# Forget gates of the recurrent mixer evicted as copies, their sigmoids taken later, and a rotation spread between index sums

## The chip, the cores and the metric

The kernel runs on one core of one Trainium2 chip. The metric is the device time of one execution in microseconds (us). The core has five engines that run their own instruction streams and wait for each other by semaphores: TensorE (PE in the profile; its weight loads are PEld), VectorE (DVE), ScalarE (ACT), GpSimd (POOL) and SyncE (SP), of which the last issues transfers only. All arithmetic is in fp32.

## What is computed

One step of two identical layers over 264 tokens: 256 of a prompt and one new token for each of 8 sequences. Each layer normalises its input, projects it by one wide matrix, and sends the parts to three mixers: a gated linear recurrence, a sparse attention whose keys an indexer picks, and an attention with compressed, selected and window keys. The part that the change touches, in short:

```
(hq, hf, hi, ..., dq, dk, dv, iq, ik, iw, ..., nq, nck, ...) = split(h @ w_in)
f   = lb + (1 - lb) * sigmoid(hf)          # forget gates, 4 heads of 128
hk  = (1 - lb) * sigmoid(-hf)
hqa = silu(hq)
dq, nq, dk, ... = rope(rms(...), qpos)     # queries and keys: root mean square, then rotation
score = sum_h iw_h * relu(iq_h . ik)       # the indexer's sum over 8 heads
```

`lb` is a bound for each channel. The rest (attention, recurrence, output gates, output projection) follows and isn't changed.

## The kernel before

Activations lie transposed, channels on the partitions and the 264 tokens in the free dimension. The projection is cut into slabs of 256 output columns (1 MB of weights each, three slots in SBUF) which stream in by SyncE's queue in a fixed order; a slot's next slab is sent when TensorE has finished the old one. Most slabs are two jobs of 128 columns. A job is 8 matmuls, shown as 16 records, into PSUM bank 0 or 1 in turn (line 902), and the job two further on may start only when ScalarE has evacuated the bank (`proj_free`). Seven slabs, among them `hf0`, are done by a scheme of seven products (line 921), whose sums VectorE forms. Everything is ordered by hand: each engine runs its own list, and every wait is written out.

The stretch around the change is the same in both layers. TensorE runs the last job pair `nq1`, the seven products of `hf0`, the sums of squares of the group `nq` (line 981), `hf1` (two jobs, heads 2 and 3 of the forget gates), `hq0` job 0, nine transposes of the values into token-major rows (line 1008, `rows`), `hq0` job 1, two transposes of the index weights (line 1016, `iw`), the first two index dots (lines 1024 and 1025), three tiny products (lines 1040 to 1043, `iwb`), `hq1` job 0, dots 2 and 3, the first key scores (line 1032), dots 4 and 5, `hq1` job 1, dots 6 and 7, and then `hi0` and `hi1` (line 914), with the recurrence's first products between them.

ScalarE meanwhile: the sigmoids of `hf0` (lines 1555 and 1557, once VectorE has formed its sums), `roots("nq")` (Ln at 1543 and Exp at 1545, which needs `zr dq`, the end of the `dq` rotation on VectorE, since both use the tile T1), then `evacuate("hf1")` (two sigmoids for each job straight out of PSUM, lines 1497 and 1498), `evacuate("hq0", 0)` (Silu, line 1523), the copies of `rows` (line 1564, recorded as 1460; their end is the mark `rows`), `evacuate("hq0", 1)`, the index weights, and the Relus of the index dots (line 1581). A function of another table set puts an ACT_TABLE_LOAD ahead of it.

VectorE: the rotation of `dq`, the rotation of `nq` in five steps (step 0 is four instructions at line 1931, steps 1 to 4 are one each at lines 1933, 1935, 1937 and 1939), then it waits for `rows`, builds small query tiles (QF at 1984 to 1986, `kn`, `vn`, QC at 1992) and `iwD` (line 1995), which `iwb` needs, and then adds up the index score, `acc 0` to `acc 7` (line 2011), each after its Relu; Relu n waits for acc n - 2. Then it scales the forget gates (lines 2032 and 2033, mark `f`), and a long chain of decays, merges and products (`decays`, `merge`, lines 2038 to 2195) gives the levels of the recurrence, with which TensorE interleaves further projection jobs.

Of the kernel before, what the change touches and what calls it, by code (L numbers as in the profile page):

```python
# [15 lines left out]
ACT = mybir.ActivationFunctionType  # L16
# [4 lines left out]
NS = 8  # L21
# [7 lines left out]
NH = 8  # L29
# [27 lines left out]
Z_IQ, Z_DQ, Z_NQ, Z_IK, Z_DK, Z_NCK, Z_NSK, Z_NWK, Z_NCV, Z_IW, Z_NWV, Z_DV, Z_NSV, Z_HQ = (  # L57
    0, 4, 8, 12, 13, 14, 15, 16, 17, 18, 19, 20, 21, 24)
# [249 lines left out]
def hybrid_step(nc, x_cols, pages_kv, page_table, state_win, win_k, win_v, state_hgrn, weights, small_w, cmp_w1,  # L308
                const, gate_rows, y_cols, z_keys, z_vals, p_hgrn, s_win, s_hgrn):
    ctx = ExitStack()  # L310
    with ctx:
# [16 lines left out]
        QC = sb("QC", [128, 2, NS * (ROWS + NH)])  # L328
# [27 lines left out]
        def at(off, *shape, rows=128):  # L356
            n = int(np.prod(shape))
            assert off + n <= ARENA, (off, shape)
            v = arena[0:rows, off:off + n]
            if len(shape) == 2:  # L360
                v = v.rearrange("p (a b) -> p a b", a=shape[0])
            if len(shape) == 3:
                v = v.rearrange("p (a b c) -> p a b c", a=shape[0], b=shape[1])
            if len(shape) == 4:
                v = v.rearrange("p (a b c d) -> p a b c d", a=shape[0], b=shape[1], c=shape[2])
            return v


        Z = at(0, NZ, LT)
# [10 lines left out]
        iwS = at(13664, NS)  # L380
        RI = at(14112, PAST // 2)
        ikT = at(14112, 4, PAST)
        iwD = at(19528, NS, NH)[0:NS]
        iwP = at(19592, 2, NH)
        i2 = at(19608, 64)[0:NS]
        SQ = (at(18208, 5, LT), at(22168, 4, LT))
        T1 = at(19528, 5, LT)
        T2 = at(20848, 5, LT)
# [5 lines left out]
        kT = at(23360, 4, LT)  # L394
        fT = at(24416, 4, LT)
# [161 lines left out]
        halves = (slice(0, HD), slice(HD, 128))  # L557
# [296 lines left out]
        def _(pe):  # L854
# [16 lines left out]
            for l in range(DEPTH):  # L871
# [139 lines left out]
                project("hq0", 1)  # L1011

                pe.wait_ge(rows_a.sem, rows_a(l, "rows"))
                pe.wait_ge(grp_v.sem, grp_v(l, "zr nq"))
                for t in range(2):
                    last = nc.tensor.transpose(ps[:, 2, t * NH:t * NH + NH], Z[0:NH, Z_IW, t * 128:t * 128 + 128], ident[0:NH, 0:NH])
                last.then_inc(pidx_p.sem, pidx_p.mark("iw"))
# [438 lines left out]
        def _(act):  # L1456
# [14 lines left out]
            for l in range(DEPTH):  # L1471
# [17 lines left out]
                def evacuate(name, only=None):  # L1489
                    for j, job in enumerate(SLAB_OF[name][2]):  # L1490
                        if only not in (None, j):
                            continue
                        n = JOB_AT[name, j]
                        act.wait_ge(proj_ready, l * NJOB + (n + 1))
                        src = ps[0:min(job[3], 128), n % 2, 0:LT]
                        if job[0] == "F":
                            A(fT[:, job[1], :], src, ACT.Sigmoid)
                            A(kT[:, job[1], :], src, ACT.Sigmoid, scale=-1.0).then_inc(proj_free, 1)  # L1498
                            continue
                        if job[0] == "S":  # L1500
                            for i in range(4):
                                last = copy(HVs[eight[i], :], ps[eight[i], n % 2, 0:128])
                            last.then_inc(proj_free, 1)
                            continue
                        if name == "ikw":
                            b, i, _ = SQUARES[Z_IK]
                            for h in halves:
                                copy(Z[h, Z_IK, :], ps[0:HD, n % 2, 0:LT])
                                A(SQ[b][h, i, :], ps[0:HD, n % 2, 0:LT], ACT.Square)
                            copy(Z[0:56, Z_IW, :], ps[HD:120, n % 2, 0:LT]).then_inc(proj_free, 1)  # L1510
                            continue
                        if job[0] == "Y":
                            copy(Y[:, job[1] // 4, job[1] % 4, :], src).then_inc(proj_free, 1)
                            continue
                        if job[1] in SQUARES and job[0] == "T":
                            b, i, group = SQUARES[job[1]]
                            copy(Z[:, job[1], :], src)
                            A(SQ[b][:, i, :], src, ACT.Square).then_inc(proj_free, 1)
                            if job[1] == (Z_NWK if group == "k" else GROUPS[group][0] + 3):
                                act.drain().then_inc(grp_a.sem, grp_a.mark(f"sq {group}"))  # L1520
                            continue
                        if job[0] == "T":
                            A(Z[0:job[3], job[1], :], src, ACT.Silu if name[:2] == "hq" else ACT.Copy).then_inc(proj_free, 1)
                            continue
                        w, o = job[3], job[4]
                        copy(HV[:, :, o:o + w], ps[:, n % 2, :].rearrange("p (t c) -> p t c", t=2)[:, :, 0:w]).then_inc(proj_free, 1)
# [11 lines left out]
                def roots(name):  # L1538

                    n = GROUPS[name][1]  # L1540
                    act.wait_ge(grp_p.sem, grp_p(l, f"ss {name}"))
                    act.wait_ge(grp_v.sem, grp_v(l, f"zr {BEFORE[name]}"))
                    A(T1[:, 0:n, :], ps[:, 2:2 + n, 0:LT], ACT.Ln, bias=epsb[:, :])
                    act.drain()
                    A(T1[:, 0:n, :], T1[:, 0:n, :], ACT.Exp, scale=-0.5).then_inc(grp_a.sem, grp_a.mark(f"rs {name}"))

                for name in FRONT[2:]:
                    if name in SEVEN:
                        squares(SEVEN.index(name))
                    elif name in SLAB_OF:  # L1550
                        evacuate(name)
                    elif name[:2] == "ss":
                        roots(name[3:])
                act.wait_ge(sv_v.sem, sv_v(l, "c 6"))
                A(kT[:, 0:2, :], fT[:, 0:2, :], ACT.Sigmoid, scale=-1.0)
                act.drain()
                A(fT[:, 0:2, :], fT[:, 0:2, :], ACT.Sigmoid)
                roots("nq")
                evacuate("hf1")
                evacuate("hq0", 0)  # L1560
                act.wait_ge(rows_p.sem, rows_p(l, "rows"))
                for t in range(3):
                    n = 128 if t < 2 else NS
# [226 lines left out]
        def _(ve):  # L1790
# [53 lines left out]
            for l in range(DEPTH):  # L1844
# [77 lines left out]
                def rotation(name, step):  # L1922

                    z, n, _, cols = GROUPS[name]
                    x, turned, kept = Z[:, z:z + n, :], T2[:, 0:n, :], T1[:, 0:n, :]
                    ve.drain()
                    if step == 0:
                        ve.wait_ge(grp_a.sem, grp_a(l, f"rs {name}"))
                        for i in range(n):
                            c = cols[i]  # L1930
                            STT(Z[:, z + i, :], Z[:, z + i, :], gains[:, c:c + 1], T1[:, i, :], ALU.mult, ALU.mult)
                    if step == 1:
                        nc.vector.stream_shuffle(turned, x, ROTATED)
                    if step == 2:
                        TT(kept, x, cosb(n), ALU.mult)
                    if step == 3:
                        TT(turned, turned, sinb(n), ALU.mult)
                    if step == 4:
                        TT(x, kept, turned, ALU.add).then_inc(grp_v.sem, grp_v.mark(f"zr {name}"))
# [31 lines left out]
                third_bank(6)  # L1971
                for step in range(1, 5):
                    rotation("dq", step)
                for step in range(5):
                    rotation("nq", step)


                ve.wait_ge(rows_a.sem, rows_a(l, "rows"))
# [3 lines left out]
                for g, h in enumerate(halves):  # L1982
                    hh = slice(4 * g, 4 * g + 4)
                    TC(qf[0:HD, 0, :, hh], Z[h, Z_IQ:Z_IQ + 4, seq_cols].rearrange("p j s -> p s j"))
                    TC(qf[h, 1, :, hh], Z[h, Z_DQ:Z_DQ + 4, seq_cols].rearrange("p j s -> p s j"))
                    TC(qf[h, 2, :, hh], Z[h, Z_NQ:Z_NQ + 4, seq_cols].rearrange("p j s -> p s j"))
                for i, z in enumerate((Z_DK, Z_NSK, Z_NWK)):
                    TC(kn[:, i, :], Z[:, z, seq_cols])
                TC(vn[:, :, :], vrow[0:NS, 2, :].rearrange("p (i c) -> p i c", i=3))
                ve.drain()  # L1990
                for a in range(2):
                    TC(QC[:, a, :].rearrange("p (b x) -> p b x", b=NS)[:, :, 0:NH], qf[:, 1 + a, :, :])
                ve.drain().then_inc(sidx_v.sem, sidx_v.mark("qf"))
                i8 = ident[0:NS, 0:NH]
                TT(iwD, Z[0:NH, Z_IW, seq_cols].unsqueeze(2).to_broadcast([NH, NS, NH]), i8.unsqueeze(1).to_broadcast([NH, NS, NH]), ALU.mult)\
# [12 lines left out]
                for n, h in enumerate(HEADS):  # L2008
                    ve.wait_ge(pidx_a.sem, pidx_a(l, f"relu {n}"))
                    for t, c in enumerate((slice(0, 128), slice(128, 384))):  # L2010
                        STT(acc[:, c], RL[:, n % 2, c], iwP[:, t, h:h + 1], causal[:, c] if n == 0 else acc[:, c], ALU.mult, ALU.add)
                    ve.drain().then_inc(pidx_v.sem, pidx_v.mark(f"acc {n}"))

                def top_keys(c):

# [506 lines left out]
```

## Time and profile before

| | |
|---|---|
| median of 3 runs | 930.22 us (929.90 to 933.64) |
| profiled execution | 933.25 us, of which the span is 931.6 us |
| TensorE busy | 912.0 us, 98% of the span |
| VectorE, ScalarE busy | 554.0 us (59%), 296.5 us (32%) |
| mean granted TensorE clock | 0.989 of full speed |
| chain that ended last, by engine | TensorE 86%, VectorE 6%, ScalarE 4% |

The busy shares say which engine has work, not what one stage waits for; the waits and the timeline of a stretch say that. In the chain that ended last each row is a piece of work and begins where the one before it released it, so rows there don't overlap. In a timeline a row is a run of like instructions of one engine, and the end of one can lie up to 0.2 us behind the start of the next, since instructions are pipelined. Square brackets give idle time of the engine before the row and what ended it. The granted clock is a share of full speed: 1.00 is 2.4 GHz and 0.50 is 1.2 GHz.

### The profile page before, as it was taken

The page shows a single profiled execution, that of the slowest core. Times are in us where ns is not written, and L with a number is a line of the kernel's source. Part 1 is how long each engine was busy: PE and PEld are TensorE (multiplying, and loading weights), DVE is VectorE, ACT ScalarE, POOL GpSimd, SP SyncE. Part 2 cuts the span into 40 slices and gives each one's busy share as a digit, 9 for nine tenths or more (in the row PEclk, how much of TensorE's full clock was granted, in tenths as well). Part 3 has the DMA queues.
Part 4 walks back from the last instruction along what each step waited for, and adds up shares of the span by engine and source line. Part 5 has one row for each costly group of instructions (what it writes and reads, how often), then busy time and mean ns, then how long its engine had stood idle before and what let it go on. Part 6 is the DMA issues. An engine that isn't in the chain of part 4 may idle for free.

```text
span 931.6 us, 18064 instructions
## 1 busy us (share of the span) xinstructions
PE 912.0 (98%) x6588; PEld 753.9 (81%) x6588; DVE 554.0 (59%) x1538; ACT 296.5 (32%) x631; POOL 130.0 (14%) x258
## 2 busy tenths in 40 slices
PE   9999899999999999999999989999999999999998
PEld 8998578878777777888899977788777777778887
DVE  5886578876744677034258755888676436751331
ACT  3134433246733113400120363422576321243000
POOL 0420000002033262000060000000110323600000
PEclk9999899999999999999999999999999999999999
DMA  8654456317189799334465443572261997973432
GB/s 293 231 171 147 155 205 258 136 57 272 46 296 381 249 386 335 116 136 156 160 197 173 162 147 121 228 269 91 92 237 56 361 384 268 381 259 140 136 135 92
DMA packets 56794, 189.05 MB, mean 203 GB/s; under 512 B 9218, under 2 KB 22914, under 8 KB 44418
## 3 DMA queue, kind: packets, MB, share of 16 engines
q1 hardware_dynamic: 43426, 138.56, 42.4%
q0 software_dynamic: 12992, 49.16, 14.1%
q8 instruction: 52, 0.85, 0.4%
q14 instruction: 36, 0.29, 0.1%
q10 hardware_dynamic: 288, 0.18, 0.1%
HBM read 177.47 MB, written 18.77 MB: 211 GB/s over the span
## 4 chain that ended last, share of the span: by engine, by line
PE 86%; DVE 6%; ACT 4%; DVEq 2%; issue 1%; ACTq 0%
PE ps L1114 18%; PE ps L902 11%; PE ps L1436 9%; PE ps L921 9%; PE ps L1330 6%; PE ps L1448 3%; PE ps L1442 3%; PE ps L914 3%; PE ps L1309 2%; PE ps L1235 2%; PE ps L1410 2%; PE ps L1224 2%; DVE arena L2091 1%; PE ps L966 1%; PE ps L1202 1%
## 5 line engine op out<-in xcount | busy, mean ns | idle before, releaser
L902 PE MATMUL ps<-hT,slab 128*128 128x264 f32 (+1 forms) x736 | 176.6, 397 | 8.8 <-ACT arena L1498 8.8
L1114 PE MATMUL ps<-hT,slab 128*128 128x264 f32 x736 | 175.8, 396 | 0.1
L902 PEld LDWEIGHTS ps<-hT,slab 128*128 128x128 f32 (+1 forms) x736 | 140.6, 194 | 35.5 <-issue 10.7
L1114 PEld LDWEIGHTS ps<-hT,slab 128*128 128x128 f32 x736 | 139.4, 193 | 30.8 <-DVEq L2245 3.2
L1460 ACT ACTIVATE arena<-ps 128x512 f32<-128x512 f32 (+21 forms) x134 | 62.6, 497 | 125.4 <-PE ps L1330 47.5
L1436 PE MATMUL ps<-Y,slab 128*128 128x264 f32 x384 | 85.8, 386 | 0.0
L1436 PEld LDWEIGHTS ps<-Y,slab 128*128 128x128 f32 x384 | 72.8, 190 | 12.3
L1330 PEld LDWEIGHTS ps<-arena,w 128*128 128x128 f32 x512 | 58.4, 192 | 10.0 <-issue 6.6
L1330 PE MATMUL ps<-arena,w 128*128 128x128 f32 x512 | 61.4, 278 | 0.0
L620 POOL DMA_DIRECT2D arena<-in_pages_kv_dram x64 | 33.4, 522 | 151.7 <-DVEq L2475 114.5
L629 POOL DMA_DIRECT2D arena<-in_pages_kv_dram x64 | 35.1, 549 | 99.6 <-PE ps L1330 27.0
L1663 ACT ACTIVATE arena<-arena,st 128x128 f32<-128x128 f32 (+1 forms) x96 | 42.4, 443 | 12.0 <-DVEq L2245 11.0
L1614 ACT ACTIVATE arena<-ps 128x264 f32<-128x264 f32 x38 | 14.8, 389 | 80.3 <-PE ps L1114 80.0
L634 POOL DMA_DIRECT2D arena<-in_pages_kv_dram x64 | 35.1, 549 | 11.7 <-PE ps L1330 9.2
L2462 DVE TENSOR_TENSOR xT<-xT,ps 128x264 f32<-128x264 f32 x16 | 6.9, 429 | 44.4 <-PE ps L1442 23.8
L1460 ACT ACTIVATE Y<-ps 128x264 f32<-128x264 f32 x24 | 9.4, 390 | 72.0 <-PE ps L902 72.0
L2099 DVE MAX8 tk<-tk 104x8 f32<-104x257 f32 x64 | 27.4, 429 | 4.3
L921 PE MATMUL ps<-arena,slab 128*128 128x132 f32 x224 | 29.8, 276 | 0.0
L1479 ACT ACTIVATE arena<-xT 128x264 f32<-128x264 f32 x16 | 6.3, 420 | 72.1 <-DVE xT L2462 67.5
L1442 PE MATMUL ps<-arena,slab 128*128 128x264 f32 x128 | 28.8, 386 | 0.0
L1448 PE MATMUL ps<-arena,slab 128*128 128x264 f32 x128 | 28.8, 386 | 0.0
L914 PE MATMUL ps<-slab,hT 128*128 128x256 f32 x128 | 28.5, 381 | 0.0
(397 smaller groups left out, 1460.1 us busy)
## 6 DMA issues: line engine op xcount, KB each, us to landing
slab<-in_weights_dram SPq DMA_DIRECT2D x84, 1024.0 KB, 5.1
arena<-in_pages_kv_dram SPq DMA_DIRECT2D x64, 256.0 KB, 8.3
arena<-in_pages_kv_dram POOLq DMA_DIRECT2D x64, 256.0 KB, 6.8
arena<-in_pages_kv_dram POOLq DMA_DIRECT2D x64, 128.0 KB, 8.3
arena<-in_pages_kv_dram SPq DMA_DIRECT2D x64, 128.0 KB, 11.9
out_dram<-in_state_win_dram POOLq DMA_DIRECT2D x2, 4088.0 KB, 24.1
arena<-in_state_hgrn_dram SPq DMA_DIRECT2D x2, 2048.0 KB, 11.6
out_dram<-arena POOLq DMA_DIRECT2D x2, 2048.0 KB, 8.9
```

The costliest lines, as they stand in the source:

```text
L629: engine.dma_start(KB[u % 4][:, e, k, :], page_of("keys", l, pages[u // 2 + NPAIR * e, 4 * (u % 2) + k])).then_inc(page_in[u % 4][odd], 16)
L634: engine.dma_start(V[:, s, i, :, :].rearrange("p a c -> p (a c)"), page_of("vals", l, pages[s, i])).then_inc(v_in[odd], 16)
L902: last = mm(ps[0:job[3], n % 2, 0:LT], v[:, k, job[2]:job[2] + job[3]], hT[:, k, :], start=(k == 0), stop=(k == KD - 1))
L914: last = mm(ps[:, n % 2, t * 256:t * 256 + width], hT[:, k, t * 128:t * 128 + 128], v[:, k, o:o + width], start=(k == 0), stop=(k == KD - 1))
L921: last = mm(out, x[:, k, :], y[:, k, :], start=(k == 0), stop=(k == 3))
L1114: last = mm(ps[:, bank, 0:LT], v[:, k, (d % 2) * 128:(d % 2) * 128 + 128], hT[:, k, :], start=(k == 0), stop=(k == KD - 1))
L1330: last = mm(out[:, kv, :, 64 * hf:64 * hf + 64], w1[:, kv, t, :], blocks[:, :, o:o + 2 * NPB8], start=(t == 0), stop=(t == ST - 1))
L1436: last = mm(ps[:, d % 4, 0:LT], v[:, j, dd * 128:dd * 128 + 128], Y[:, a, j, :], start=(j == 0), stop=(j == 3))
L1442: last = mm(ps[:, 4 + d, 0:LT], views[d // 2][:, k, (d % 2) * 128:(d % 2) * 128 + 128], mT[:, k, :], start=(k == 0), stop=(k == KD - 1))
L1448: last = mm(ps[:, d - 4, 0:LT], v[:, k, (d % 2) * 128:(d % 2) * 128 + 128], mT[:, k, :], start=(k == 0), stop=(k == KD - 1))
L1460: return A(out, in_, ACT.Copy, scale=scale)
L1663: A(x[:, j, :], x[:, j, :], ACT.Exp, scale=-1.0, bias=st[:, c + j:c + j + 1], accum_out=sa[:, c + j:c + j + 1])
```

## The change

- ScalarE copies `hf1` raw out of PSUM into the tile fT in place of four sigmoids. The copy of job 0 stands ahead of `roots("nq")`, that of job 1 behind it.
- The sigmoids of `hf0` are not taken ahead of the roots. All four heads are taken at once (kT from fT with scale -1, then fT in place, 128x1056 each), behind the Silu of `hq0` job 0 and ahead of the copies of `rows`.
- VectorE does steps 0 and 1 of the `nq` rotation where it did all five. Steps 2 and 3 go behind `acc 1`, and step 4 behind `acc 5`, followed by the QF copies of `dq` and `nq` and the two QC copies that were made ahead of `iwD`.
- TensorE doesn't wait for the end of the `nq` rotation (`zr nq`) ahead of the `iw` transposes, and `iwD`, `iwP` and `i2` move to a place in the arena that the rotation doesn't use.

```diff
@@ buffers
-        iwD = at(19528, NS, NH)[0:NS]
-        iwP = at(19592, 2, NH)
-        i2 = at(19608, 64)[0:NS]
+        iwD = at(30000, NS, NH)[0:NS]
+        iwP = at(30064, 2, NH)
+        i2 = at(30080, 64)[0:NS]
@@ TensorE
                 pe.wait_ge(rows_a.sem, rows_a(l, "rows"))
-                pe.wait_ge(grp_v.sem, grp_v(l, "zr nq"))
@@ ScalarE, evacuate
                         if job[0] == "F":
-                            A(fT[:, job[1], :], src, ACT.Sigmoid)
-                            A(kT[:, job[1], :], src, ACT.Sigmoid, scale=-1.0).then_inc(proj_free, 1)
+                            copy(fT[:, job[1], :], src).then_inc(proj_free, 1)
                             continue
@@ ScalarE, order
+                evacuate("hf1", 0)
+                roots("nq")
+                evacuate("hf1", 1)
+                evacuate("hq0", 0)
                 act.wait_ge(sv_v.sem, sv_v(l, "c 6"))
-                A(kT[:, 0:2, :], fT[:, 0:2, :], ACT.Sigmoid, scale=-1.0)
                 act.drain()
-                A(fT[:, 0:2, :], fT[:, 0:2, :], ACT.Sigmoid)
-                roots("nq")
-                evacuate("hf1")
-                evacuate("hq0", 0)
+                A(kT, fT, ACT.Sigmoid, scale=-1.0)
+                act.drain()
+                A(fT, fT, ACT.Sigmoid)
                 act.wait_ge(rows_p.sem, rows_p(l, "rows"))
@@ VectorE
-                for step in range(5):
-                    rotation("nq", step)
+                rotation("nq", 0)
+                rotation("nq", 1)
                 ...
                     TC(qf[0:HD, 0, :, hh], Z[h, Z_IQ:Z_IQ + 4, seq_cols].rearrange("p j s -> p s j"))
-                    TC(qf[h, 1, :, hh], Z[h, Z_DQ:Z_DQ + 4, seq_cols].rearrange("p j s -> p s j"))
-                    TC(qf[h, 2, :, hh], Z[h, Z_NQ:Z_NQ + 4, seq_cols].rearrange("p j s -> p s j"))
                 ...
-                ve.drain()
-                for a in range(2):
-                    TC(QC[:, a, :].rearrange("p (b x) -> p b x", b=NS)[:, :, 0:NH], qf[:, 1 + a, :, :])
                 ve.drain().then_inc(sidx_v.sem, sidx_v.mark("qf"))
                 ...
                     ve.drain().then_inc(pidx_v.sem, pidx_v.mark(f"acc {n}"))
+                    if n == 1:
+                        rotation("nq", 2)
+                        rotation("nq", 3)
+                    if n == 5:
+                        rotation("nq", 4)
+                        ve.drain()
+                        for g, h2 in enumerate(halves):
+                            hh = slice(4 * g, 4 * g + 4)
+                            TC(qf[h2, 1, :, hh], Z[h2, Z_DQ:Z_DQ + 4, seq_cols].rearrange("p j s -> p s j"))
+                            TC(qf[h2, 2, :, hh], Z[h2, Z_NQ:Z_NQ + 4, seq_cols].rearrange("p j s -> p s j"))
+                        ve.drain()
+                        for a in range(2):
+                            TC(QC[:, a, :].rearrange("p (b x) -> p b x", b=NS)[:, :, 0:NH], qf[:, 1 + a, :, :])
```

## Rows read from the trace of the kernel before

**Rows 1.** Busy time and share of every engine, from the page
```profile
PE 912.0 (98%) x6588; PEld 753.9 (81%) x6588; DVE 554.0 (59%) x1538; ACT 296.5 (32%) x631; POOL 130.0 (14%) x258
```

**Rows 2.** Waits of TensorE: total us, times, longest
```profile
PE ps L902 <- ACT arena L1498: 8.8, 2, 4.4
PE ps L1093 <- DVEq L2195: 2.0, 2, 1.0
```

**Rows 3.** Chain that ended last, 66 to 145 us: start us, us, what
```profile
97.88 6.14 PE ps L902 x16
104.01 0.98 PE ps L1008 x9
104.99 3.56 PE ps L902 x16
108.56 0.22 PE ps L1016 x2
...
109.64 0.20 PE ps L1040 x2
...
132.47 6.91 PE ps L914 x32
```

**Rows 4.** Timeline of TensorE: start us, busy us, line, operation, count, idle before
```profile
86.20 7.28 PE L902 MATMUL ps<-hT,slab 128*128 128x264 f32 x32
```

**Rows 5.** Timeline of ScalarE, layer 0, same columns
```profile
90.89 1.28 ACT L1543 ACT_TABLE_LOAD   x1 [4.21 <-DVE arena L1939]
...
94.67 1.08 ACT L1545 ACTIVATE arena<-arena 128x1056 f32<-128x1056 f32 x1
...
98.32 1.28 ACT L1523 ACT_TABLE_LOAD   x1
104.05 0.39 ACT L1523 ACTIVATE arena<-ps 128x264 f32<-128x264 f32 x1 [4.45 <-PE ps L902]
105.03 1.22 ACT L1460 ACTIVATE arena<-ps 128x384 f32<-128x384 f32 x3 [0.59 <-PE ps L1008]
```

**Rows 6.** Timeline of VectorE, layer 0, same columns
```profile
95.78 1.71 DVE L1931 SCALAR_TENSOR_TENSOR arena<-arena,small 128x264 f32<-128x264 f32 x4 [4.97 <-ACT arena L1545]
...
101.67 1.26 DVE L1939 TENSOR_TENSOR arena<-arena 128x1056 f32<-128x1056 f32 x1
106.34 0.06 DVE L1796 MEMSET spare<- 128x1 f32 x1 [3.41 <-ACTq L1565]
...
107.58 0.34 DVE L1989 COPY vn<-arena 8x384 f32<-8x384 f32 x1
...
108.41 0.21 DVE L1995 TENSOR_TENSOR arena<-arena,cst 8x64 f32<-8x64 f32 x1
...
115.43 1.61 DVE L2011 SCALAR_TENSOR_TENSOR arena<-arena 128x128 f32<-128x128 f32 x4 [2.57 <-ACT arena L1581]
...
121.92 1.61 DVE L2011 SCALAR_TENSOR_TENSOR arena<-arena 128x128 f32<-128x128 f32 x4 [3.01 <-ACT arena L1581]
```

**Rows 7.** TensorE in windows of 1 us: busy, granted clock, DMA share, GB/s
```profile
96.00:97.00 1.00, 0.00 (x0) 0.50 1.00 426
...
102.00:103.00 1.00, 1.00 (x5) 0.69 0.00 0
...
202.00:203.00 1.00, 0.50 (x3) 1.00 0.00 0
...
297.00:298.00 1.00, 1.00 (x3) 0.59 1.02 357
```

**Rows 8.** Timeline of TensorE around two thin stretches of layer 0
```profile
202.50 0.31 PE L1183 MATMUL ps<-cst,arena 104*128 104x104 f32 x1 [0.71 <-ACT arena L1460]
...
294.32 1.93 PE L1282 MATMUL ps<-arena 15*64 15x512 f32 x8
...
296.94 5.51 PE L1114 MATMUL ps<-hT,slab 128*128 128x264 f32 x16
```

**Rows 9.** Timeline of the SyncE queue: start us, us, line, transfer
```profile
108.59 0.33 SPq L688 DMA_DIRECT2D slab<-in_weights_dram  x1
```

## The prediction

> **What bounds the kernel now.** I read the page first. TensorE is busy 98% of the span, so only its idle time, its time at the lower clock and its own work can give anything [rows 1]. The waits of TensorE come next, and nearly half of its 20 us of idle time is one wait: job 0 of `hq0` waits for ScalarE's second sigmoid of `hf1`, line 1498, twice (once a layer), 4.4 us each [rows 2]. The next largest is 1.0 us a layer. Third, the chain that ended last, around that wait: the job behind the wait takes 6.14 us, where the same 16 records take 3.56 us a little later [rows 3]. The windows of 1 us say why: the granted clock is 0.50 (1.2 GHz) from 96 us on, after TensorE stood still from 93.5 us, and full (2.4 GHz) again within the window 102 to 103 [rows 7]. So the wait costs 4.39 us of standing and 2.58 us of slow matmuls, about 7.0 us a layer, 14 us in all.
>
> What ended the wait is ScalarE's timeline. It can't take the roots of `nq` before 90.89 us, because the `dq` rotation holds T1; two table loads, Ln and Exp follow and end at 94.67 + 1.08 = 95.75; and only then come a third load and the sigmoids that free bank 1 [rows 5]. But job 0 of `hf1` had been done since 86.20 + 3.56 = 89.76 us [rows 3, 4], with ScalarE idle for 4.21 us until 90.89 [rows 5].
>
> **The change part by part** (times of layer 0; layer 1 has the same shape).
>
> *Copies in place of sigmoids.* The copy of `hf1` job 0 (0.39 us, as the 128x264 Silu [rows 5]) fits into the idle 4.21 us, at 89.8 to 90.2. It frees bank 1, and `hq0` job 0 starts straight behind `hf1`, at 86.20 + 2 x 3.56 = 93.32, in place of 97.88. At full clock it ends at 96.88. The `rows` transposes wait for the roots (95.75), which is earlier, and end at 96.88 + 0.98 = 97.86; `hq0` job 1 follows and ends at 97.86 + 3.56 = 101.42 [rows 3]. Its bank is free at 96.2. In the trace of before it ended at 108.56, so TensorE is 7.14 us ahead here, which is the 4.39 and the 2.58 and 0.17 of overlap between matmuls.
>
> *What is late next: ScalarE's `rows`.* The work taken from ahead of the wait now stands ahead of the `rows` copies. From 95.75: copy of `hf1` job 1 0.39; load for Silu 1.28; Silu 0.39; load for Sigmoid 1.28; two sigmoids of 128x1056, each as the Exp of that shape, 1.08; three copies of `rows` 1.22 [rows 5]. The sum is 6.72 us, and two drains make it about 6.8: `rows` is marked at about 102.55 us (before: 105.03 + 1.22 = 106.25 [rows 5]). TensorE comes to its wait for it at 101.42, so a new wait of about 1.15 us takes the place of the old one. Queued behind it on TensorE are `iw` and the first dots, 109.64 - 108.56 = 1.08 us [rows 3], which end at 103.7.
>
> *VectorE's small tiles.* `iwb` needs `iwD`. Before, it was done at 108.41 + 0.21 = 108.62, 2.37 us after `rows` [rows 5, 6]. The change takes four of six QF copies from that path (the six, a memset and part of `kn` fill the 1.24 us from 106.34 to 107.58, some 0.12 each with a gap saved, so 0.5 us) and the QC copies with their drain (from 107.92 to 108.41 is 0.49, of which a drain of 0.1 stays) [rows 6]. That leaves about 1.5 us: `iwD` at 102.55 + 1.5 = 104.05, another wait of about 0.35 us. `iwb` then starts at about 104.1 in place of 109.64. **The shift is 5.5 us a layer, 11.0 us in all.** Rotation steps 0 and 1 end at 95.78 + 1.71 + 1.33 = 98.8, well ahead of `rows`, and taking away the wait for `zr nq` gives nothing in itself: the rotation would have ended by 101.67 + 1.26 = 102.93 [rows 6], 0.4 us behind `rows`.
>
> *The third load.* `hq0` job 1 now needs a Silu load again, behind `rows`: 102.6 + 1.28 + 0.39 = 104.3 [rows 5]. That is before `iwb` is out, so the Relus, which wait for `iwb`, don't move against it.
>
> *Deferred steps.* Steps 2 and 3 of the rotation are 2 x 1.33 = 2.7 us (1.26 and a gap) behind `acc 1`, where VectorE sat idle 2.57 us before `acc 2`; and Relu 4, the first that needs `acc 2`, waits for TensorE longer than the 0.1 us left over. Step 4, four copies and two QC copies are 1.3 + 0.6 + 0.4 = 2.3 us behind `acc 5`, where the idle time before `acc 6` was 3.01 us [rows 6]. Both are hidden. Without this cover the 5.0 us would go to the mark `f` and from there to the chain of levels, which is what TensorE waits for at line 1093, 1.0 us a layer [rows 2]. With the cover, `f` moves by the same 5.5 us as TensorE, and so does all that follows; the transfers are sent on TensorE's marks and move with it. The slab of `hi1` is sent on the end of `hq0`, so at 101.4 in place of 108.59 [rows 9], 7.1 us earlier, for a use that moves from 132.5 by 5.5 (the row of line 914) [rows 3]; the 16 index-key transfers behind it on SyncE's queue gain as much.
>
> *Edits that cost nothing:* new addresses for `iwD`, `iwP` and `i2` add no wait.
>
> *The clock.* This is the unknown term. From 101.4 to about 104.7 us TensorE would have no dense matmul: 1.15 us of waiting, 1.1 us of 8-row and 64-row products, 0.35 us of waiting, 0.6 us of tiny products. The clock fell after the wait of 4.39 us; it also fell with no wait at all, at 297 us, behind 2.5 us of products with 15 and 24 rows, and the job at 296.94 took 5.51 us, where one of this shape takes half of 7.28, so 1.9 us more [rows 4, 7, 8]. It did not fall at 202 to 203 us, where thin products and 0.71 us of waiting make a stretch of about the same length [rows 7, 8]. So the new stretch costs 0 to 1.9 us a layer. The same fall at 297 us was there in both layers of this execution. It may be gone in another, which would give up to 3.8 us back, and that the profiled execution is 3.03 us above the median fits this, though only one trace shows it. Against the profiled 933.25 us the sum is thus 933.25 - 11.0 = 922.25, with 0 to 3.8 us to add and 0 to 3.8 to take off; against the median, 930.22 - 11.0 = 919.2 with 0 to 7.6 to add. I take one low stretch, 1.9 us: 921.1 us. The stretches at 202 us and at 297 us are about equally near to the new one, so about half of the places is what I go by, less one, as the median execution seems to have had none at 297 us.
>
> *A rule against the change.* The trace shows 1.28 us for each table load, with the next ACTIVATE right behind it [rows 5], and the change puts Silu, Sigmoid and Silu in a row, two more switches than grouping would need. The Trainium skill, "ScalarE: Activation LUTs", section "What ACT_TABLE_LOAD costs", counts a drain of about 1.38 us beside each load of 1.28 us, and its rules say to do all of one set before switching. By the page the two loads ahead of `rows` would cost 2.76 us a layer more and the sum would be an estimated 926.6. The trace doesn't agree: from 90.89 to 94.67 are 3.78 us for a load, an Ln of the Exp's size and a second load, 1.28 + 1.1 + 1.28, which leaves 0.1 us for drains [rows 5].
>
> **The rivals.**
> *1. ScalarE is later than summed.* Each microsecond by which `rows` is late is one on TensorE, since TensorE waits for it already. If what stands ahead of `rows` costs two more table loads' worth, 2 x 1.28 = 2.6 us a layer, the result is 921.1 + 5.1 = 926.2. Against it: every piece has its own duration in the rows, and the loads are all 1.28 us. The table rule of the page is of this kind.
> *2. Clock low in most places.* All four possible low stretches (the new one and that at 297 us, in each layer) give 919.2 + 7.6 = 926.8; three give 924.9. For it: the new stretch is longer than either row that I compare it with. Against it: the one at 202 us did nothing.
> *3. Slower: the clock stays low.* The place is from `iwb` on. At 0.50 each microsecond of full-speed matmuls costs one more, so from 5.5 us of them at the lower clock a layer gains nothing. If it stayed low through both `hq1` jobs and `hi0`, some 14 us of such work, a layer would lose 8.5 us, and the result would be 947. Against it: the longest low stretch in the rows is from 96 to 102.6 us, and it ended under dense matmuls, as these are.
> *4. No effect.* The wait only moves: the level chain on VectorE, busy throughout, is as late as before, because the deferred 5.0 us land in it. Then a layer gains 5.5 - 5.0 = 0.5 us, and the result is 929 to 930. Against it: the idle times of 2.57 and 3.01 us [rows 6].
> *5. More.* The sigmoids or small tiles cost less, and no low stretch comes: 916 to 918.5.
>
> **How the numbers follow.** Forecast, 919 to 923.5 (none to two low stretches): 0.62. Rival 1: 0.08. Rival 2: 0.13. Rival 3: 0.02. Rival 4: 0.06. Rival 5: 0.09. The predicted time is 921.1. The range 918.0 to 926.0 holds the forecast, the three-stretch case and about half of rivals 1 and 5, a little over 0.8. A measurement of this kernel can tell about 0.5% (4.65 us) from no change: faster means below 925.6. Faster: 0.62 + 0.09 + most of rival 2 and half of rival 1 = 0.86. Within: 0.11. Slower: 0.03.
>
> **What the profile after would show.** The wait of `hq0` on ScalarE gone; `hq0` job 0 straight behind `hf1` in 3.56 us; a wait of about 1.2 us at line 1016 ended by ScalarE's `rows` copies and one of about 0.35 us at line 1040 ended by VectorE; `acc 2` and `acc 6` not later against their Relus; the granted clock around 102 to 109 us either full or with one low stretch that costs up to 1.9 us; the wait at line 1093 still 1.0 us. The prediction is wrong if `rows` comes after about 103.5 us, if Relu 4 or 6 waits for VectorE, or if the level chain starts to hold TensorE for longer.

## The result and the profile after

| | before | after |
|---|---|---|
| median | 931.93 us (929.90 to 935.99, 4 runs) | 922.48 us (919.95 to 924.44, 4 runs) |
| profiled execution | 933.25 us, span 931.6 | 921.3 us, span 919.6 |
| mean granted TensorE clock | 0.989 | 0.998 |
| TensorE busy | 912.0 us | 905.0 us |

The ratio is 0.9883, with a 95% interval of 0.9853 to 0.9913: some 11 us faster (8 to 14 us by the interval; the medians of the table are 9.4 us apart). Two more comparisons of the same kernel, on other occasions, gave 0.9875 (0.9850 to 0.9901) and 0.9864 (0.9833 to 0.9895).

The waits of TensorE after the change (engine and line, what it waited for: us in total, times, longest). The line numbers of TensorE's part are one lower than before.

```profile
PE ps L1092 <- DVEq L2203: 2.1, 2, 1.1
PE ps L1015 <- ACTq L1565: 1.8, 2, 0.9
...
PE ps L1039 <- DVE arena L1990: 0.7, 2, 0.3
```

The 8.8 us of [rows 2] are gone. In their place stand two short waits: at the `iw` transposes for ScalarE's mark `rows`, 0.9 us a layer, and at `iwb` for VectorE's `iwD`, 0.34 us. The wait in the level chain is what it was, 1.0 us a layer [rows 2].

The timeline of TensorE in layer 0. In this execution the layer begins 0.65 us later than in the one of before (86.85 against 86.20 [rows 4]), so 0.65 is to be taken off each time:

```profile
86.85 10.84 PE L902 MATMUL ps<-hT,slab 128*128 128x264 f32 x48
97.53 1.15 PE L1008 MATMUL ps<-cst,arena 128*128 128x128 f32 x9
98.51 3.73 PE L902 MATMUL ps<-hT,slab 128*128 128x264 f32 x16
103.15 0.29 PE L1015 MATMUL ps<-cst,arena 8*128 8x8 f32 x2 [0.91 <-ACTq L1565]
...
104.64 0.27 PE L1039 MATMUL ps<-arena,cst 8*8 8x64 f32 x2 [0.34 <-DVE arena L1990]
...
105.26 3.83 PE L902 MATMUL ps<-hT,slab 128*128 128x264 f32 x16
```

The same timeline of the kernel before, from `hq0` job 0 on:

```profile
97.88 6.14 PE L902 MATMUL ps<-hT,slab 128*128 128x264 f32 x16 [4.39 <-ACT arena L1498]
...
109.57 0.27 PE L1040 MATMUL ps<-arena,cst 8*8 8x64 f32 x2
...
110.19 3.83 PE L902 MATMUL ps<-hT,slab 128*128 128x264 f32 x16
```

After the change the first row is 48 records long: both jobs of `hf1` and job 0 of `hq0` run in one piece, 10.84 us, at full clock. Before, `hq0` job 0 alone took 6.14 us behind 4.39 us of waiting. `iwb` starts at 104.64 - 0.65 = 103.99 in place of 109.57, a shift of 5.58 us a layer. `hq1` job 0 behind it is 5.58 us earlier too (105.26 - 0.65 = 104.61 in place of 110.19). The chain [rows 3] puts `iwb` of before at 109.64; only timelines are compared here.

ScalarE in the same stretch:

```profile
90.61 0.39 ACT L1459 ACTIVATE arena<-ps 128x264 f32<-128x264 f32 x1 [8.96 <-PE ps L902]
91.52 1.28 ACT L1541 ACT_TABLE_LOAD   x1 [0.52 <-DVE arena L1939]
...
95.30 1.08 ACT L1543 ACTIVATE arena<-arena 128x1056 f32<-128x1056 f32 x1
96.29 0.38 ACT L1459 ACTIVATE arena<-ps 128x264 f32<-128x264 f32 x1
96.69 1.28 ACT L1521 ACT_TABLE_LOAD   x1
97.98 0.39 ACT L1521 ACTIVATE arena<-ps 128x264 f32<-128x264 f32 x1
98.44 1.28 ACT L1558 ACT_TABLE_LOAD   x1
99.73 1.08 ACT L1558 ACTIVATE arena<-arena 128x1056 f32<-128x1056 f32 x1
100.88 1.08 ACT L1560 ACTIVATE arena<-arena 128x1056 f32<-128x1056 f32 x1
101.87 1.20 ACT L1459 ACTIVATE arena<-ps 128x384 f32<-128x384 f32 x3
103.17 1.28 ACT L1521 ACT_TABLE_LOAD   x1
```

The first copy sits in 8.96 us of idle time, where before the sigmoids of `hf0` and a table load stood. From the end of the roots (95.30 + 1.08) to the end of the copies of `rows` (101.87 + 1.20) it is a queue 6.7 us long, with no gap over 0.1 us, of which 2.56 us are table loads. Each ACTIVATE begins 0.01 us behind its load.

And VectorE's index sums with the deferred steps between them:

```profile
107.18 0.75 DVE L2006 SCALAR_TENSOR_TENSOR arena<-arena 128x128 f32<-128x128 f32 x2
108.10 1.26 DVE L1935 TENSOR_TENSOR arena<-arena,cst 128x1056 f32<-128x1056 f32 x1 [0.17 <-issue]
109.44 1.26 DVE L1937 TENSOR_TENSOR arena<-arena,cst 128x1056 f32<-128x1056 f32 x1
110.62 3.36 DVE L2006 SCALAR_TENSOR_TENSOR arena<-arena 128x128 f32<-128x128 f32 x8
114.16 1.26 DVE L1939 TENSOR_TENSOR arena<-arena 128x1056 f32<-128x1056 f32 x1 [0.17 <-issue]
...
116.15 0.38 DVE L2020 COPY QC<-QF 128x64 f32<-128x64 f32 x2
116.99 1.61 DVE L2006 SCALAR_TENSOR_TENSOR arena<-arena 128x128 f32<-128x128 f32 x4 [0.46 <-ACT arena L1581]
```

`acc 2` to `acc 5` run in one piece (3.36 us, eight records) straight behind rotation steps 2 and 3: of the idle 2.57 us ahead of `acc 2` [rows 6] nothing is left, and `acc 2` comes 5.46 us earlier than before where TensorE is 5.58 us earlier, so 0.12 us late. Ahead of `acc 6` 0.46 us of the 3.01 us of idle time [rows 6] are left. The deferred steps fit, with little to spare.

### The profile page after: what moved, and what is told of

It is laid out like the page before. It is cut to its first block, busy times and chain, and to the rows that moved or that the text cites. A ratio compares the mean times of both kernels' runs of the same rounds, so it can differ in the third digit from the quotient of the medians.

```text
span 919.6 us, 18062 instructions
## 1 busy us (share of the span) xinstructions
PE 905.0 (98%) x6588; PEld 750.0 (82%) x6588; DVE 553.8 (60%) x1538; ACT 297.1 (32%) x627; POOL 129.7 (14%) x258
## 4 chain that ended last, share of the span: by engine, by line
PE 84%; DVE 7%; ACT 3%; DVEq 2%; issue 2%; DMA 1%; ACTq 0%; SPq 0%
PE ps L1113 18%; PE ps L902 9%; PE ps L1435 9%; PE ps L921 9%; PE ps L1329 7%; PE ps L1447 3%; PE ps L1441 3%; PE ps L914 3%; PE ps L1308 2%; PE ps L1234 2%; PE ps L1409 2%; PE ps L1223 2%; DVE arena L2099 1%; PE ps L1201 1%; PE ps L891 1%
## 5 line engine op out<-in xcount | busy, mean ns | idle before, releaser
L902 PE MATMUL ps<-hT,slab 128*128 128x264 f32 (+1 forms) x736 | 171.4, 389 | 0.0
L902 PEld LDWEIGHTS ps<-hT,slab 128*128 128x128 f32 (+1 forms) x736 | 137.7, 190 | 24.4 <-issue 1.1
L1459 ACT ACTIVATE arena<-ps 128x512 f32<-128x512 f32 (+12 forms) x138 | 64.1, 494 | 142.6 <-PE ps L1329 47.2
```

The costliest lines, as they stand in the source:

```text
L902: last = mm(ps[0:job[3], n % 2, 0:LT], v[:, k, job[2]:job[2] + job[3]], hT[:, k, :], start=(k == 0), stop=(k == KD - 1))
L1459: return A(out, in_, ACT.Copy, scale=scale)
```

## The experiments

My theory: the copy of `hf1` job 0 ahead of the roots takes away a wait and with it the lower clock behind it; what is left is set, one for one, by what stands ahead of ScalarE's `rows` and of VectorE's `iwD`. All ratios are to the kernel before, timed beside them. The runs follow the theory's steps. Rows are of layer 0 unless it is said otherwise.

**The change again.**

> The change itself, once more, as the yardstick of the runs beside it. About 9 to 11 us below the kernel before (0.988 to 0.990). Its trace should again show the two new waits, 0.91 us at the iw transposes and 0.34 us at iwb, a layer.

Measured: 921.03 us against 932.95, 0.9875 (0.9850 to 0.9901), at the good end of what was expected. The waits are 1.8 and 0.7 us in all, as above.

**The wait parted from the clock.** The kernel before, with nine spare products in the wait, whose results nothing uses:

```diff
                 project("hf1", 1)
+                for _ in range(9):
+                    mm(ps[:, 7, 0:LT], ident, hT[:, 0, :], start=True, stop=True)
                 project("hq0", 0)
```

> The kernel before, with nine spare 264-column products into the unused bank 7 behind hf1, about 4.0 us of work in the wait of 4.39 us (results unused). It parts the price of the wait from that of the lower clock. My theory: the clock stays at 2.4 GHz, hq0 job 0 takes 3.6 us in place of 6.14, and the time falls by 2 x 2.5 = 5 us, to about half of the gain of the change, with no wait taken away. The rival, the slow job has another cause (banks, transfers): no gain, or a small loss if the spare products run past the wait.

Measured: 928.68 us against 932.85, 0.9942 (0.9919 to 0.9964), 4 to 5 us faster with nine products more in each layer (18 records). The timeline of its TensorE:

```profile
87.67 7.28 PE L902 MATMUL ps<-hT,slab 128*128 128x264 f32 x32
94.80 4.17 PE L1003 MATMUL ps<-hT,cst 128*128 128x264 f32 x18
99.35 3.80 PE L902 MATMUL ps<-hT,slab 128*128 128x264 f32 x16 [0.39 <-ACT arena L1500]
```

Job 0 of `hq0` starts 11.68 us behind the start of `hf1` (99.35 - 87.67), to the hundredth as before (97.88 - 86.20 [rows 4]), since ScalarE has not changed. But it takes 3.80 us in place of 6.14. The mean granted clock of this execution is 1.000, against 0.989. The lower clock was thus a cost of its own, 2.3 us a layer, and the cause was TensorE standing still. About 5 of the change's 11 to 12 us are this.

**The two halves of the change.** First ScalarE's half alone (VectorE's list as before: five rotation steps, six QF copies and two QC copies ahead of `iwD`; the new addresses and the removed wait stay).

```diff
-                rotation("nq", 0)
-                rotation("nq", 1)
+                for step in range(5):
+                    rotation("nq", step)
```

> The change with VectorE's list put back: all five steps of the nq rotation, all QF and QC copies ahead of iwD. My theory: ScalarE's part frees the bank and carries the gain; VectorE's part is only there to keep iwD early. rows comes at about 102.5 us but the rotation ends about 0.5 us later, then 2.3 us to iwD in place of 1.45 us: iwb 1.3 us a layer later than in the change, 2.6 us in all, so about 8 us below the kernel before. Rival A, the moved passes carry a good part of the gain: less than 5 us below before. Rival B, they give nothing: as the change.

Measured: 927.4 us (924.2 to 932.9) against 932.95, 0.9931 (0.9909 to 0.9954). That is 5.5 us, half of the change's gain, less than the 8 us that I expected, and nearer to the bound that I had set for rival A. The timeline of its TensorE, and the windows of 1 us (length, busy, granted clock, DMA share, GB/s):

```profile
103.09 0.29 PE L1015 MATMUL ps<-cst,arena 8*128 8x8 f32 x2 [0.92 <-ACTq L1565]
...
105.81 0.38 PE L1039 MATMUL ps<-arena,cst 8*8 8x64 f32 x2 [1.57 <-DVE arena L1995]
...
106.74 6.63 PE L902 MATMUL ps<-hT,slab 128*128 128x264 f32 x16
```

```profile
104.00:105.00 1.00, 0.24 (x4) 1.00 0.98 352
105.00:106.00 1.00, 0.19 (x2) 0.81 0.93 385
106.00:107.00 1.00, 1.00 (x9) 0.50 0.85 286
...
112.00:113.00 1.00, 1.00 (x5) 0.78 0.13 35
```

The second wait is 1.57 us, 1.23 more than in the change, as the theory has it. But the clock fell here, behind two waits of 0.92 and 1.57 us with thin products between them, in both layers: `hq1` job 0 took 6.63 us in place of 3.83, so 2.8 us more on top of 1.23, and the tiny products ahead of it another 0.3 us. This execution took 932.9 us; the best one, 924.2 us, was 8.7 us below before, as expected without that fall. Its mean granted clock was 0.998, that of the other two 0.993. An estimate: one stretch at half clock as long as the one here (6.8 us) takes 0.0037 off the mean, and one as short as that at 297 us before (3.4 us) 0.0018. This profile has two of each kind (0.989), and two short ones alone would leave 0.996, so 0.993 needs at least one of the long ones. The fall was thus in three of the four executions.

VectorE's half alone (the kernel before, with VectorE's list, the addresses and the removed wait of the change):

> The kernel before with VectorE's part of the change, the new addresses and no wait for zr nq, and ScalarE's list as before. My theory: nothing, within 0.3 us of before, since before the change iwD was done 1 us ahead of TensorE and the rotation 3 us ahead of rows. The rival, the shorter path to iwD or the removed wait is worth something on its own: 1 to 2 us faster; or the deferred steps cost something: slower by up to 6 us.

Measured: 932.73 us against 932.85, 1.000 (0.9983 to 1.0018). Its TensorE waits at `hq0` as before:

```profile
PE ps L902 <- ACT arena L1497: 8.8, 2, 4.4
```

Nothing, as expected. VectorE's half is worth nothing by itself and about half of the gain beside the other, part of it by the clock, since it decides only when `rows` is early. The deferred steps cost nothing either.

**What sets the new waits.** Twice more sigmoids ahead of `rows`:

```diff
                 A(kT, fT, ACT.Sigmoid, scale=-1.0)
                 act.drain()
+                A(kT, fT, ACT.Sigmoid, scale=-1.0)
+                act.drain()
+                A(kT, fT, ACT.Sigmoid, scale=-1.0)
+                act.drain()
                 A(fT, fT, ACT.Sigmoid)
```

> The change with the sigmoid of kT done three times over (same result), 2 x 1.15 us more ahead of the rows copies. My theory of one for one: the wait at iw grows from 0.91 to about 3.2 us a layer, 4.6 us in all, and since TensorE then stands for over 3 us, the clock falls there too and costs up to 1.9 us more a layer: 4.6 to 8.4 us above the change. The rival, that the new wait has slack in what follows (the level chain on VectorE sets the end anyway): less than 3 us above the change.

Measured: 931.4 us against 932.85, 0.9982 (0.9968 to 0.9996), so 10 us above the change by the ratios, more than the 4.6 to 8.4 that I expected. Its TensorE in layer 0:

```profile
105.29 0.28 PE L1015 MATMUL ps<-cst,arena 8*128 8x8 f32 x2 [3.22 <-ACTq L1569]
...
107.66 6.80 PE L902 MATMUL ps<-hT,slab 128*128 128x264 f32 x16
```

The wait grew from 0.91 to 3.22 us, which is one for one with 2.3 us of work, and the job behind it took 6.80 us in place of 3.83. The two together are 5.3 us a layer. The price of the clock, 3 us, is over the upper end that I had given, 1.9 us, and this is what the expectation had too small.

Less work ahead of `rows`: the sigmoids of `hf0` stay in the idle time ahead of the roots, and only heads 2 and 3 are taken late.

```diff
+                act.wait_ge(sv_v.sem, sv_v(l, "c 6"))
+                A(kT[:, 0:2, :], fT[:, 0:2, :], ACT.Sigmoid, scale=-1.0)
+                act.drain()
+                A(fT[:, 0:2, :], fT[:, 0:2, :], ACT.Sigmoid)
                 evacuate("hf1", 0)
                 roots("nq")
                 ...
-                act.wait_ge(sv_v.sem, sv_v(l, "c 6"))
                 act.drain()
-                A(kT, fT, ACT.Sigmoid, scale=-1.0)
+                A(kT[:, 2:4, :], fT[:, 2:4, :], ACT.Sigmoid, scale=-1.0)
                 act.drain()
-                A(fT, fT, ACT.Sigmoid)
+                A(fT[:, 2:4, :], fT[:, 2:4, :], ACT.Sigmoid)
```

> The change, but the sigmoids of hf0 (heads 0 and 1) stay where they were, in ScalarE's idle time ahead of the roots, and only heads 2 and 3 are taken behind the Silu, 128x528 each (0.64 us) in place of 128x1056 (1.08 us). My theory: what stands ahead of the rows copies sets the new wait one for one, so it shrinks by 0.88 us a layer, from 0.91 to about 0.05, and the time by 1.8 us against the change. The rival, the wait is set by something else (the transposes, a drain, a table load): no change.

Measured: 918.91 us (918.38 to 919.34) against 932.95, 0.9850 (0.9834 to 0.9867), 2.1 us below the change beside it. In layer 0:

```profile
102.18 0.29 PE L1015 MATMUL ps<-cst,arena 8*128 8x8 f32 x2 [0.36 <-ACTq L1568]
```

The wait fell from 0.91 to 0.36 us in layer 0, and in layer 1 nothing but a gap of 0.04 us is left of it, as expected. In layer 0 of this execution the roots began 0.33 us later, counted from `hf1` (91.43 - 86.43 = 5.00 us, against 91.52 - 86.85 = 4.67 in the change), and 0.91 - 0.88 + 0.33 is 0.36. So the wait follows the queue to the hundredth, and taking all four heads at once is the part of the change that costs something. Why the roots began later here stays open.

All four sigmoids behind Relu 1, and the evacuation of `hq1` job 0 behind Relu 5:

```diff
                 evacuate("hq0", 0)
-                act.wait_ge(sv_v.sem, sv_v(l, "c 6"))
-                act.drain()
-                A(kT, fT, ACT.Sigmoid, scale=-1.0)
-                act.drain()
-                A(fT, fT, ACT.Sigmoid)
                 act.wait_ge(rows_p.sem, rows_p(l, "rows"))
                 ...
                 relus(1)
-                evacuate("hq1", 0)
+                act.wait_ge(sv_v.sem, sv_v(l, "c 6"))
+                act.drain()
+                A(kT, fT, ACT.Sigmoid, scale=-1.0)
+                act.drain()
+                A(fT, fT, ACT.Sigmoid)
                 for n in range(2, 6):
                     relus(n)
+                evacuate("hq1", 0)
                 evacuate("hq1", 1)
```

> The change, but all four sigmoids stand behind Relu 1, with rows copied straight behind the first Silu, and hq1 job 0 evacuated behind Relu 5. The count of table loads stays. My theory: both new waits go (0.91 and 0.34 us a layer), 2.5 us below the change, so 11.5 to 13.5 us below the kernel before, and the chance of a low clock behind them goes too. The rival, the wait moves again: Relus 2 to 5 now wait for the sigmoids, and acc and the dots with them, which gives the 2.5 us back or more.

> The change again in five rounds, beside the kernel with late sigmoids on the same chip: 0.986 to 0.990 of before.

> The kernel with late sigmoids again in five rounds. My theory: 2.5 us below the change beside it (the two new waits of 1.25 us a layer gone), 0.983 to 0.987 of before. The rival, that the first result was luck in where the clock fell: as the change, within 1 us.

Measured: 917.96 us and 0.9846 (0.9824 to 0.9867) in the first comparison. In the second, of more rounds, it was 916.85 us and 0.9814 (0.9786 to 0.9841), beside 920.68 us and 0.9864 for the change. It beats both kernels: 3 to 4 us below the change, where 2.5 us were expected; the intervals of the two kernels overlap a little in both comparisons. The timeline of TensorE, from the first comparison, has no wait between `hf1` and `hi0`:

```profile
85.95 10.84 PE L902 MATMUL ps<-hT,slab 128*128 128x264 f32 x48
96.63 1.15 PE L1008 MATMUL ps<-cst,arena 128*128 128x128 f32 x9
97.61 3.73 PE L902 MATMUL ps<-hT,slab 128*128 128x264 f32 x16
101.27 0.29 PE L1015 MATMUL ps<-cst,arena 8*128 8x8 f32 x2
...
102.35 0.27 PE L1039 MATMUL ps<-arena,cst 8*8 8x64 f32 x2
...
102.97 3.83 PE L902 MATMUL ps<-hT,slab 128*128 128x264 f32 x16
...
115.27 7.17 PE L914 MATMUL ps<-slab,hT 128*128 128x256 f32 x32
```

And that of `hi0` in the change:

```profile
117.38 7.17 PE L914 MATMUL ps<-slab,hT 128*128 128x256 f32 x32
```

From the start of `hf1` to that of `hq1` are 17.02 us, against 18.41 in the change and 23.99 before, so 1.4 us a layer less than in the change. Up to `hi0` they are 29.32 us, against 30.53: 0.2 us are given back at dots 4 and 5, and 1.2 us a layer, 2.4 in all, stay. That is the size that was expected; the rest of the 3 to 4 us is within the intervals.

**The cover of the deferred steps.** In the change, rotation steps 2 to 4 and the copies in one piece behind `acc 7`, ahead of the mark `f`:

> The change with VectorE's deferred steps 2 to 4 and the copies put behind acc 7 in one piece, where no idle time covers them: 4.9 us straight ahead of the mark f. My theory: f is 4.9 us later, of which some 2 us are slack ahead of the first recurrence products and the chain of levels; the rest, about 3 us a layer, appears as waits of TensorE in the levels: about 6 us above the change. The rival that the chain of levels has more slack than that: within 1 us of the change. The rival that it has none: 10 us above, so no gain over the kernel before.

Measured: 928.87 us against 932.85, 0.9954 (0.9934 to 0.9974), so 7 to 8 us above the change. The waits of its TensorE:

```profile
PE ps L1062 <- DVEq L2042: 5.6, 2, 2.9
PE ps L1092 <- DVEq L2202: 2.1, 2, 1.1
```

A wait of 2.8 us a layer appeared at line 1062, the recurrence's first products, which need `f`. The levels, line 1092, wait for no longer than before. So the size was right, 5 us of work less 2 us of slack, and the place was not: I had put it into the chain of levels. The lower clock came behind this wait as well:

```profile
127.99 3.44 PE L1062 MATMUL ps<-arena 128*128 128x128 f32 x16 [2.94 <-DVEq L2042]
...
585.53 3.78 PE L1062 MATMUL ps<-arena 128*128 128x128 f32 x16 [2.71 <-DVEq L2042]
...
589.10 8.38 PE L914 MATMUL ps<-slab,hT 128*128 128x256 f32 x32
```

In the change the products of line 1062 take 2.05 us and the job pair behind them 7.07. So the clock cost 1.4 us in layer 0 and 1.7 + 1.3 = 3.0 us in layer 1. With the waits that is 10.1 us, where the span of this execution is 9.4 us above that of the change beside the first experiments (928.9 against 919.5): the wait and the clock account for all of it.

## Why the prediction was right, point by point

The forecast was 921.1 us, within 918 to 926; the median came out at 922.48. The mechanism was right; that the number came so near is in part luck, as the last points say.

- **What bounds.** Right. The one wait of 4.39 us and the slow job behind it were what the change took away, and the spare products showed the two prices apart, 2.3 us for the clock against the 2.58 that I read.
- **The shift.** 5.5 us a layer forecast, 5.58 measured, and so still at the first products of the recurrence (125.50 - 0.65 in place of 130.42). Job 0 of `hq0` starts straight behind `hf1`.
- **ScalarE late next.** The sum of 6.72 us plus drains was 6.7 us in the trace. The wait was forecast at 1.15 us and is 0.91; I counted 0.1 us for drains that overlap the next work, and a job by the 3.56 us of the chain, though its end as TensorE's next wait sees it is 0.17 later. The experiments with more and with less in the queue moved the wait the way the sum has it.
- **VectorE's small tiles.** 0.35 us forecast, 0.34 measured.
- **Deferred steps.** Covered, as forecast, but for the 0.12 us of `acc 2`, which reached no wait of TensorE: 0.46 us of cover were left ahead of `acc 6`, where I had 0.7. The idle time ahead of Relus 4 and 6 is ended by TensorE, after 1.00 and 0.46 us, as before. Rival 4 (no effect) needed them to land in the level chain, whose wait is 1.0 us a layer as before. What happens without cover was right in size and wrong in place.
- **The clock.** This term was kept open, and one low stretch was taken. In the profiled execution of the change the only one was again behind the 15-row and 24-row products, in layer 0, and the new place had none in the three profiled executions of the change. The other two had no low stretch at all. Over all 14 timed executions of the change the mean granted clock was 0.996 to 1.000, where four low stretches gave 0.989 with ScalarE's half alone, so rival 2 (low in most places) is out. The 1.9 us that I charged to the new place are thus shown by no run of the change. The upper end was too low besides: where the clock does fall in the new place, the job behind it costs 2.7 to 3.0 us, not 1.9, since the clock then stays low for longer (from about 105.6 to 112.4 us with ScalarE's half alone, against 297.2 to 300.6 before). The nearer row was that of the wait itself, 96 to 102.6 us and 2.58 us, which I had read. Why a stretch is short or long stays open: with the deferred steps uncovered, the same products behind nearly the same wait met a low stretch of 3.4 us in layer 0 and of 6.8 us in layer 1.
- **The base.** 930.22 us was low for the kernel before; further runs gave medians of 931.9 to 933.7. It was 1.7 us below the median of the first comparison, and the 1.9 us for a low stretch made up for it by luck. The 9.1 us of gain that the forecast has from it compare with 9.4 between the medians of the first comparison and 12 to 13 in the two later ones, and the shift by itself, 2 x 5.58 = 11.2 us, is nearer to these.
- **The rule on table switches.** The Trainium skill, "ScalarE: Activation LUTs", section "What ACT_TABLE_LOAD costs", would put 1.38 us of drain beside each load of 1.28 us. The loads here take 1.28 us, each begins within 0.1 us of the end of the ACTIVATE before it, and the next ACTIVATE starts 0.01 us behind, so the trace doesn't agree on the drain. The advice of its section "Rules for kernel authors", to do all of one set before switching, was not tested by a kernel with fewer loads. But the late-sigmoid kernel has as many loads as the change and the kernel before (42), the one with two and two heads has 44, and both are faster than the change: here it mattered more where a load stands than how many there are.

Rival 3 (slower) needed the lower clock to cost 5.5 us a layer. The clock did fall in the new place in the profiles of two variants, where it cost some 3 us a layer, about half of that, and rose again under dense matmuls. In the profiles of the change it didn't fall there. Rival 5 (more than forecast, 916 to 918.5 us) isn't what came, nor is rival 1: `rows` was marked within 0.15 us of the forecast.

## What to carry to other kernels

A bank is freed by its copy, not by what is to be computed from it: if an evacuating engine has a long function queued behind a wait, copy first and compute in place later. No run parts the copy of job 0 from its new place ahead of the roots. By the rows, an estimate: its two sigmoids take 0.67 us (97.06 to 97.73 in the kernel before), ScalarE still had the table of the sigmoids of `hf0`, and from 89.96 us on they would have ended at 90.6, ahead of the roots at 90.89. So for job 0 the order may be enough; job 1 ends too late for that. Work that is moved off a wait is late somewhere else; find the next mark on that engine's queue (here `rows`) and put the work behind it if another gap is to be had, which was worth another 3 to 4 us here. Waits of about 1 us were cheap one by one, but two of them with thin products between can take TensorE's clock with them: in the profile of ScalarE's half alone 1.2 us more of waiting cost 4 us a layer.

## What the runs showed that I had not expected

The granted clock fell to 0.50 (1.2 GHz) though no wait was longer than 1.57 us: 0.92 us of waiting, 1.15 us of products with 64 rows and 8x8 transposes, and 1.57 us of waiting, in both layers of one execution. With about 0.9 and 0.34 us in the same places the three profiled executions of the change kept 1.00 there. In the first of them:

```profile
102.00:103.00 1.00, 0.24 (x2) 1.00 1.00 412
103.00:104.00 1.00, 0.85 (x10) 1.00 0.86 148
104.00:105.00 1.00, 0.66 (x8) 1.00 0.83 311
```

Executions of the change in one comparison lie 4 to 5 us apart. Some of it is the number of low stretches (none or one in its profiles, four in those of the kernel before), but two with the same mean clock of 0.998 took 919.95 and 924.44 us. Single late transfers are another part: in some executions TensorE waits for the window keys, 3.3 us in all in that of the spare products and 1.3 us in one of the change, and in others not at all.
